# Second block: the norms of queries and keys and the decay's scalars between the projection's products

## What is computed

```python
def hybrid_layer(x, ln1_g, w_in, q_norm_g, k_norm_g, rpb, ...):
    h = rms_norm_2(x, ln1_g)
    proj = h @ w_in                                # 3*512 attention, 4*512 delta rule, 16 scalars
    aq, ak, av, dqkv, dz, dab = jnp.split(proj, ...)
    aq = rms_norm_2(hs(aq), q_norm_g)              # per head of 64
    ak = rms_norm_2(hs(ak), k_norm_g)
    attn = rms_norm_2(neighbourhood_attention(aq, ak, hs(av), rpb), attn_out_g)
    dn = bidirectional_gated_deltanet(dqkv, dz, dab[:, :, 0], dab[:, :, 1], conv_w, ...)
    x = x + jnp.concatenate([attn, dn], axis=-1) @ w_out
    return x + hierarchical_moe(rms_norm_2(x, ln2_g), ...)

# inside the delta rule's mixer
    qkv = silu(conv(qkv_raw, width 5, per channel))
    q = l2_norm(q) * 128 ** -0.5; k = l2_norm(k)   # per head of 128
    g = -exp(a_log) * softplus(a + dt_bias); beta = sigmoid(b)
    o = rms_norm_2(gated_delta_rule(both directions), out_norm_g) * silu(z)
```

## Time and profile before

| | us |
|---|---|
| median of 3 runs | 2851.36 |
| lowest, highest | 2849.64, 2853.24 |
| the profiled execution | 2852.15 |
| span in its profile | 2850.4 |
| mean granted clock over the span | 0.858 |
| PE busy | 2314.1 (81%) |
| DVE busy | 1195.0 (42%) |
| ACT busy | 855.3 (30%) |
| POOL busy | 190.0 (7%) |

### The profile page before, as it was taken

One profiled execution on the slowest core, in us unless ns is written; L12 is line 12 of the kernel. 1 busy time (PEld: TensorE's weight loads), 2 busy tenths in 40 slices (PEclk: granted clock), 3 DMA queues, 4 the chain that ended last, 5 costly groups with the idle time before them and its releaser, 6 DMA issues. The chain is left out here.

```text
span 2850.4 us, 32608 instructions
## 1 busy us (share of the span) xinstructions
PE 2314.1 (81%) x13804; PEld 1694.5 (59%) x13804; DVE 1195.0 (42%) x1868; ACT 855.3 (30%) x1270; POOL 190.0 (7%) x190
## 2 busy tenths in 40 slices
PE   7889999958964667679999979867688588888884
PEld 5768888837822667458888858646676533333331
DVE  3346664374158444546664344434524411111112
ACT  4324443264242222334443243464103210101000
POOL 0000000000004111000000000000220011111100
PEclk9889999979986666789999989965757699999997
DMA  4112232222200110122222223210104199999996
GB/s 182 60 59 89 89 104 82 95 76 97 79 0 4 18 15 13 60 74 76 102 98 87 98 72 119 84 28 1 23 1 164 78 388 419 416 408 407 401 396 233
DMA packets 106597, 377.27 MB, mean 132 GB/s; under 512 B 54960, under 2 KB 55744, under 8 KB 67536
## 3 DMA queue, kind: packets, MB, share of 16 engines
q1 hardware_dynamic: 84848, 296.44, 28.1%
q10 hardware_dynamic: 9216, 67.11, 5.7%
q0 software_dynamic: 12384, 11.58, 1.4%
HBM read 375.31 MB, written 27.53 MB: 141 GB/s over the span
## 5 line engine op out<-in xcount | busy, mean ns | idle before, releaser
L579 PE MATMUL ps<-xh,wh 128*128 128x512 f32 x1384 | 552.8, 399 | 85.9 <-DVE wl L546 35.9
L580 PE MATMUL ps<-xl,wh 128*128 128x512 f32 x1384 | 548.1, 396 | 0.0
L581 PE MATMUL ps<-xh,wl 128*128 128x512 f32 x1384 | 547.4, 396 | 0.0
L546 DVE TENSOR_TENSOR wl<-raw,wh 128x2048 fp32r<-128x2048 f32 (+2 forms) x127 | 264.4, 2082 | 326.4 <-ACT wh L540 326.4
L579 PEld LDWEIGHTS ps<-xh,wh 128*128 128x128 f32 x1384 | 266.1, 192 | 159.7 <-issue 55.3
L2959 PE MATMUL ps<-egu,XT 128*64 128x512 f32 x1088 | 272.1, 657 | 84.5 <-DMA egu<-e_up 80.1
L581 PEld LDWEIGHTS ps<-xh,wl 128*128 128x128 f32 x1384 | 265.6, 192 | 56.4
L580 PEld LDWEIGHTS ps<-xl,wh 128*128 128x128 f32 x1384 | 266.4, 192 | 54.9
L540 ACT ACTIVATE wh<-raw 128x2048 fp32r<-128x2048 f32 (+2 forms) x127 | 220.3, 1735 | 82.7 <-PE ps L864 69.3
L2959 PEld LDWEIGHTS ps<-egu,XT 128*64 128x64 f32 x1088 | 94.8, 151 | 238.3 <-issue 222.3
L2977 DVE TENSOR_TENSOR HIDT<-ps,SIL 128x256 f32<-128x256 f32 x34 | 14.4, 424 | 350.1 <-ACT SIL L2969 350.1
(11 more groups left out here) (460 smaller groups left out, 3385.7 us busy)
## 6 DMA issues: line engine op xcount, KB each, us to landing
egu<-e_gate SPq DMA_DIRECT2D x68, 1024.0 KB, 14.5
egu<-e_up SPq DMA_DIRECT2D x68, 1024.0 KB, 25.5
ed<-e_down ACTq DMA_DIRECT2D x64, 1024.0 KB, 9.7
raw<-up SPq DMA_DIRECT2D x44, 1024.0 KB, 4.8
raw<-down SPq DMA_DIRECT2D x32, 704.0 KB, 4.0
raw<-rwkv_rkv SPq DMA_DIRECT2D x12, 1024.0 KB, 4.8
raw<-in_dn SPq DMA_DIRECT2D x8, 1024.0 KB, 4.8
raw<-sgu_u SPq DMA_DIRECT2D x4, 1024.0 KB, 8.3
```

What stands on the lines that cost most here:

```text
L546: e.tensor_tensor(K.WL[s][:, 0:n], K.RAW[r][:, 0:n], K.WH[s][:, 0:n].bitcast(F32), SUB).then_inc(*K.w_low.mark(i))
L579: e.matmul(o, h[:, q, k], x_high[:, k], start=k == 0, stop=False)
L580: e.matmul(o, h[:, q, k], x_low[:, k], start=False, stop=False)
L581: last = e.matmul(o, l[:, q, k], x_high[:, k], start=False, stop=k == KT - 1)
```

## The change

- PE: the 8 norm products of queries and keys stand between the two value chunks; the 16 scalar columns come before the delta tiles; the transposes of the scalars after delta tiles 0 and 1; the 8 norm products of the delta rule's q and k after tile 11; the decay's products between tiles 13 and 14. Tiles 12 to 15 (the gate) come last.
- ACT: the square of a query or key tile follows its copy; the 8 logarithms stand between the two value chunks, the 8 exponentials after them; the square of a delta q or k tile follows its silu; sigmoid and two exponentials stand after tile 4; all other logarithms and exponentials between tile 11 and the gate.
- DVE: the norm of query or key tile m follows the convolution of tile m; the scalars' first steps follow tile 2, the rest stands before the norms of the delta rule's q and k.
- The squares have rooms of their own (`square_room`), in buffers that are filled later; the convolutions turn over 5 temporary tiles in place of 6.
- SP and POOL: bias tile 0 has another room and is loaded after the first query tile; bias tiles 1 to 3 and the second half of the values' tiles wait for delta tile 15, the last product.
- `gemm_pe` and `gemm_tok_pe` can make a part of a stage's tiles.

```diff
@@ weights, uses
         feed("in2_v", 2048)
+        feed("in2_ab", 1024)
         feed("in2_dn", 2048)
-        feed("in2_ab", 1024)
...
-                        ("n_fin", 1), ("n_ln1", 1), ("in2_qk", 8), ("in2_v", 8), ("in2_dn", 16), ("in2_ab", 2),
-                        ("sq_qk", 8), ("sq_kq", 8), ("dn_sc", 1)):
+                        ("n_fin", 1), ("n_ln1", 1), ("in2_qk", 8), ("in2_v0", 4), ("sq_qk", 8), ("in2_v1", 4), ("in2_ab", 1), ("in2_dn", 2),
+                        ("ab_turned", 1), ("in2_dn2", 10), ("sq_kq", 8), ("in2_dn12", 2), ("dn_sc", 1), ("in2_dn14", 2)):
@@ layer2_sp, layer2_pool
+    e.wait_ge(*K.gemm_sum("in2_qk", 0))
+    load_bias(K, e, 0)
     load_weights(K, e, K.first["in2_dn"], K.first["out2"])
-    e.wait_ge(*K.gemm_sum("in2_ab", 0))
-    for b in range(4):
+    e.wait_ge(*K.gemm_sum("in2_dn", 15))
+    for b in range(1, 4):
+        load_bias(K, e, b)
...
         if b == 2:
-            e.wait_ge(*K.gemm_sum("in2_ab", 0))
+            e.wait_ge(*K.gemm_sum("in2_dn", 15))
@@ layer2_pe
     gemm_pe(K, e, "in2_qk", "in2_qk", 8, K.XH, K.XL)
-    gemm_tok_pe(K, e, "in2_v", "in2_v", 2, 256, "in2_qk")
-    gemm_pe(K, e, "in2_dn", "in2_dn", 16, K.XH, K.XL, ready="in2_qk")
+    gemm_tok_pe(K, e, "in2_v", "in2_v", range(1), 256, "in2_qk")
+    squares_pe(K, e, "sq_qk", "blk")
+    gemm_tok_pe(K, e, "in2_v", "in2_v", range(1, 2), 256, "in2_qk")
     gemm_pe(K, e, "in2_ab", "in2_ab", 1, K.XH, K.XL, mt=1, ready="in2_qk")
+    gemm_pe(K, e, "in2_dn", "in2_dn", 2, K.XH, K.XL, ready="in2_qk")
...
+    gemm_pe(K, e, "in2_dn", "in2_dn", 10, K.XH, K.XL, ready="in2_qk", begin=2)
+    squares_pe(K, e, "sq_kq", "ones")
+    gemm_pe(K, e, "in2_dn", "in2_dn", 2, K.XH, K.XL, ready="in2_qk", begin=12)
...
+    gemm_pe(K, e, "in2_dn", "in2_dn", 2, K.XH, K.XL, ready="in2_qk", begin=14)
@@ layer2_act
+        e.wait_ge(*K.act_out("in2_qk", m))
+        e.activation(square_room(K, "sq_qk", m), K.QK[:, m], ACT.Square).then_inc(*K.square.mark("sq_qk", m))
...
+    values(0)
+    factors_ln_act(K, e, "sq_qk")
+    values(1)
+    factors_exp_act(K, e, "sq_qk")
+    next_high(K, e, K.first["in2_ab"])
...
         e.activation(dst, z, ACT.Silu).then_inc(*K.act_out.mark("in2_dn", m))
+        if m < 8:
+            e.wait_ge(*K.act_out("in2_dn", m))
+            e.activation(square_room(K, "sq_kq", m), of_kq(K, m), ACT.Square).then_inc(*K.square.mark("sq_kq", m))
+        if m == 4:
+            e.wait_ge(*K.dve_delta("abs"))
+            e.activation(K.sc["BE"][:, :, :, :], of_ab(K, 1), ACT.Sigmoid).then_inc(*K.act_delta.mark("beta"))
+            e.activation(flat(K, "SC2"), flat(K, "SC2"), ACT.Exp, scale=-1.0).then_inc(*K.act_delta.mark("exp"))
...
+    factors_ln_act(K, e, "sq_kq")
+    factors_exp_act(K, e, "sq_kq")
@@ layer2_dve
         K.board.empty(u, K.conv("in2_dn", m, 3))
+        if m < 8:
+            e.wait_ge(*K.rstd("sq_qk", m, "r"))
+            e.scalar_tensor_tensor(K.QK[:, m], K.QK[:, m], K.prm("qg" if m < 4 else "kg"), square_room(K, "sq_qk", m), MUL, MUL).then_inc(
+                *K.normed.mark("sq_qk", m))
```

More of the change, by code:

```diff
@@ L556, in next_low, with gemm_pe @@
         weight_low(K, e, i + 1)
-def gemm_pe(K, e, name, stage, nm, x_high, x_low, mt=2, at=0, ready=None):
-    for i in range(nm // mt):
+def gemm_pe(K, e, name, stage, nm, x_high, x_low, mt=2, at=0, ready=None, begin=0):
+    use = K.u[stage if begin == 0 else f"{stage}{begin}"] - begin
+    for i in range(begin // mt, (begin + nm) // mt):
         item = K.first[name] + at + i
@@ L573, in gemm_pe @@
             for q in range(mt):
-                u = K.u[stage] + mt * i + q
+                u = use + mt * i + q
                 o = K.ps[:, u % 8]
@@ L587, in gemm_tok_pe @@
 def gemm_tok_pe(K, e, name, stage, chunks, cols, ready):
-    for ch in range(chunks):
+    for ch in chunks:
         item = K.first[name] + ch
@@ L1837, in layer2_pool, with squares_pe @@
             e.dma_start(K.AVB[b][:, half], src).then_inc(*K.v_in[b].landing(b, half))
+def squares_pe(K, e, name, of):
+    for m in range(8):
+        u = K.u[name] + m
+        for t in K.board.emptied(u - 8):
+            e.wait_ge(*t)
+        e.wait_ge(*K.square(name, m))
+        e.matmul(K.ps[:, u % 8], K.cst(of, 128), square_room(K, name, m), start=True, stop=True).then_inc(*K.norm_sum.mark(name, m))
 def layer2_pe(K, e):
@@ L1871, in layer2_pe, with ab_room, square_room, dn_use @@
     e.matmul(K.ps[:, b, 96:128], K.cst("half", 128, 128), GG, start=True, stop=True).then_inc(*K.delta_sum.mark("decay"))
+    gemm_pe(K, e, "in2_dn", "in2_dn", 2, K.XH, K.XL, ready="in2_qk", begin=14)
 def of_kq(K, m):
     return K.KQ[:, 1 - m // 4, m % 4]
+def ab_room(K):
+    return K.GT[0:16, 0].rearrange("p a b -> p (a b)")
+def square_room(K, name, m):
+    if name == "sq_qk":
+        return K.DV[:, m] if m < 4 else K.ZG[:, m - 4]
+    if m < 4:
+        return K.AT[:, m]
+    if m < 6:
+        return K.GT[:, m - 4].rearrange("p a b -> p (a b)")
+    return K.EX[:, :] if m == 6 else K.T[5]
+def dn_use(K, m):
+    at = 0 if m < 2 else 2 if m < 12 else 12 if m < 14 else 14
+    return K.u[f"in2_dn{at}" if at else "in2_dn"] + m - at
+def factors_ln_act(K, e, name):
+    for m in range(8):
+        u = K.u[name] + m
+        e.wait_ge(*K.norm_sum(name, m))
+        e.activation(square_room(K, name, m), K.ps[:, u % 8], ACT.Ln, bias=K.prm("eps"), scale=1.0 / 64 if name == "sq_qk" else 1.0).then_inc(
+            *K.rstd.mark(name, m, "ln"))
+        K.board.empty(u, K.rstd(name, m, "ln"))
+def factors_exp_act(K, e, name):
+    for m in range(8):
+        x = square_room(K, name, m)
+        e.wait_ge(*K.rstd(name, m, "ln"))
+        e.activation(x, x, ACT.Exp, scale=-0.5).then_inc(*K.rstd.mark(name, m, "r"))
 def layer2_act(K, e):
@@ L1947, in layer2_act @@
     e.activation(K.EH[:, :, :].rearrange("p a b -> p (a b)"), K.ps[:, b, 64:128], ACT.Exp).then_inc(*K.act_delta.mark("eh"))
+    K.board.empty(K.u["dn_sc"], K.act_delta("eh"))
     e.activation(flat(K, "EG"), flat(K, "GC"), ACT.Exp).then_inc(*K.act_delta.mark("eg"))
     e.activation(flat(K, "ED"), flat(K, "GL"), ACT.Exp).then_inc(*K.act_delta.mark("ed"))
+    for m in range(12, 16):
+        u = dn_use(K, m)
+        e.wait_ge(*K.gemm_sum("in2_dn", m))
+        e.wait_ge(*K.normed("sq_qk", m - 8))
+        e.activation(K.ZG[:, m - 12], K.ps[:, u % 8], ACT.Silu).then_inc(*K.act_out.mark("in2_dn", m))
+        K.board.empty(u, K.act_out("in2_dn", m))
     K.board.point("ACT", "attn")
@@ L1977, in layer2_dve @@
         next_low(K, e, K.first["in2_v"] + i)
-    for m in range(16):
+    next_low(K, e, K.first["in2_ab"])
+    u = K.u["in2_ab"]
+    e.wait_ge(*K.gemm_sum("in2_ab", 0))
+    e.tensor_copy(ab_room(K), K.ps[0:16, u % 8]).then_inc(*K.dve_out.mark("in2_ab"))
+    K.board.empty(u, K.dve_out("in2_ab"))
+    full = {k: K.sc[k][:, :, :, :] for k in K.sc}
+    for m in range(12):
         if m % 2 == 0:
             next_low(K, e, K.first["in2_dn"] + m // 2)
-        if m >= 12:
-            continue
-        u = K.u["in2_dn"] + m
-        z, o = K.T[m % 6], K.ps[:, u % 8]
+        u = dn_use(K, m)
+        z, o = K.T[m % 5], K.ps[:, u % 8]
         e.wait_ge(*K.act_out("in2_dn", m, "tap"))
@@ L2019, in layer2_dve @@
+    next_low(K, e, K.first["in2_dn"] + 6)
     e.wait_ge(*K.act_delta("ln"))
```

124 lines of the change are left out of this document (43 added, 81 removed).

## The result

The changed kernel takes **2826.37 us** (median of 4 executions, 2809.28 to 2829.09); the kernel before takes 2851.23 on the same chip. The ratio is 0.990, 95% interval 0.986 to 0.994. The profiled execution took 2829.09 us (span 2827.3), so it is 2.7 above the median.

What follows compares the result with a forecast made beforehand. It took a serial norms stretch before attention, and ACT and DVE pacing the projection, as the bounds. -58.5 + 16.8 PE work + 28.1 waits + 4.6 clock - 2 attention = -11.0, so 2840.5 us; range 2832.5 to 2848.

Steps and rivals of the forecast that it cites:

- the last term: Attention's start: PE arrives at full clock, so the first 4 us of its work run faster; -2 us, bounds 0 and 4.
- Rival B: Attention stays at full clock: -21 us in place of -2, 2822 us in all; chance 0.07.
- The serial stretch taken away: Norms and decay between projection and attention, 50.6 us, go, with 7.9 us of old projection waits; together -58.5 us.
- Ring of 13.5 per pair: Projection of the delta rule's features: squares lengthen the ACT and DVE cycle per tile pair by 1.34, to 13.5 us.
- Rival A: In the projection, the squares don't lengthen the ACT and DVE cycle: -17.9 us, 2833 us in all; chance 0.06.
- The pair with three loads: Behind tile 4, sigmoid, two exponentials and three table loads add 4.5 us, making that pair 18.0 us, PE wait 7.2.
- Ring waits, 15.1: Projection: PE's waits at tile pairs lengthened by squares, small activations and table loads; together 15.1 us.
- Clock, +4.6 for three falls: Projection: PE's clock falls to 0.50 at three long waits, 1.5 us each; +4.6 us.
- Norm products, 13.9: 16 norm products return to PE between the projection's products at 0.87 us each; 13.9 us.
- Decay 2.3: The decay's small products return to PE between the projection's products; 2.3 us.
- C: Rival: the pauses of each pair lose PE's clock in the projection; +38 us, 2879 in all; chance 0.05.
- D: Rival: no change to speak of; the projection's cycle grows 1.3 us more per pair; -2.6 us, 2848.5 in all; chance 0.10.

Runs made afterwards that it cites:

- after_kept_warm: Changed kernel with 8 extra PE products without use in the pause ahead of each of attention's first three blocks' row transposes; 2807.89 us.
- after_cold: Changed kernel with 12 more silus of the last gate tile on ACT, 8 us in which PE idles ahead of attention; 2844.40 us.
- after_decay_last: Changed kernel with the decay's products and the three following exps put back behind the gate's last tiles; 2832.49 us.
- before_warm: Kernel before with 20 PE products without use between the last norm product and the wait for the decay's rates; 2845.77 us.
- before_carried: Kernel before with 22 PE products without use ahead of the decay's products and 4 between these and attention; 2843.96 us.
- after_ring_short: Changed kernel with ACT's sigmoid and two exps moved from behind tile 4 to behind the casting of tile 12's weights; 2827.24 us.
- after_norms_twice: Changed kernel with each of the 16 norm products issued twice; 2833.35 us.
- after_again: The changed kernel run once more without an edit, for its spread; 2828.04 us, one execution of six at 2805.65.
- after_filled_waits: Changed kernel with PE products without use in the projection's waits ahead of several delta tiles and the keys' last norm product; 2829.39 us.

## Why the prediction was wrong

**The step that failed** is the last term, "I take 2; bounds 0 and 4" for attention's start. It measured 10.75 us. The value was taken from the earlier trace rows, where a stretch of small products lost the clock near 979 us with PE busy 2.09 of 3.40 us. Attention after the change is busy 15.07 of 23.50, about the same share, and kept it. The row was read as a property of sparse products in general; it was one place, with other shapes (64x64 and 128x64). And the bounds weren't bounds: "the first 4 us of its work" had no row behind it. From the rows that were shown, the block of 34.27 us up to the pause of 3.93 and PE's busy share of 82% gave a price for the whole block at full clock: half of 0.82 x 34.3 = 28 us of PE work at most, 14, and that was the upper bound to put in.

**Rival B** named the mechanism with 0.07: full clock up to the first long pause. Its sign came true: attention's clock is 0.61 over the 105 us from 1879. I had held the fall near 979 against it. The Trainium skill ("TensorE: Matmul & The Clock Gate", section "Why this matters for your kernels") says that PE-idle gaps over some 3 us bring the clock down. Here the trace agrees at the first pause (4.36 us: clock lost; filled: clock kept, after_kept_warm), and in after_cold (8.24). It isn't the whole: the clock was also lost in or right behind waits of 1.62, 1.70 and 2.17 us in after_decay_last, before_warm and before_carried, so the absence of a long gap is no promise. My doubt had that much ground; the value and the bounds that I drew from it had none. B's own price, 21 us more, was too large, as it took all of attention; only the first block stays warm, 10.75.

**The forecast sum without that term** was -9.0 at attention's start; measured -13.0 there, -13.7 from the stage's start, and -13.2 from there with attention entered at full clock in both. Its steps:

- *The serial stretch taken away, -58.5*: held. Nothing of it is left in the stage rows.
- *Ring of 13.5 per pair*: 13.52 and 13.51. Right, and after_ring_short shows the ring by moving what is in it. Rival A is out. *The pair with three loads, 18.0*: 16.70; the third load (1806.52) lies under a convolution of DVE.
- *Wait before the first delta tiles, 4.8*: 4.72. *Keys' last product, 2.8*: 2.48. *Tile 12, 4.5*: 3.63. *End, 0.9*: 0.69. Right within a microsecond each.
- *Ring waits, 15.1*: 8.5 (2.28 + 0.73 + 5.52). With them the waits are 20.1, not 28.1. *Clock, +4.6 for three falls*: there were four stretches at 0.50, of 3.4, 3.4, 6.8 and 6.8 us. These two terms count one thing twice: where the ring paces, PE at 0.50 works into its own wait, so the waits are shorter and the falls nearly free. With most of the falls filled away (the clock at 0.99) the stage got 1.2 us shorter, and 1.6 came from the first fall alone, which stands outside the ring. There were more falls than I had, and so the double count and the miscount partly cancel.
- *Norm products, 13.9*: the queries' half is on the path (after_norms_twice: 6.8 us for eight more, 0.85 each). The keys' half has 6.1 us of waits right behind it, which it could have been set against. *Decay 2.3*: 1.0 (1866.13 to 1867.16), since it now runs at full clock.
- The 4.7 us by which the stage came out better are then 1.3 (the third load), 1.3 (decay) and 1.5 (the four small waits), and 0.6 in what doesn't cancel above. This split is an estimate; only the loads, the norm products and the clock falls were moved by a run of their own.
- *Bias and value tiles cost nothing*: right. DMA share is 0.70 in the first 23.5 us of attention, and no wait of PE names them. PE is idle 0.69 us between the stages, as forecast under 2.
- *C, slower by a lost clock in the projection*: the clock does fall there, 4 times. The first fall costs 1.6 us, near the 1.5 of the forecast, and the one behind tile 4 nothing, for the reason above; what the last two cost no run shows one by one. *D* is out by the 13.5.
- Small slips that change nothing: 2851.36 - 11.0 is 2840.4, not 2840.5, and the sum without falls, -17.6, is 2833.8, while the range starts at 2832.5.

So with the fills in both kernels the change is worth 9.7 us. That this is near the 11 forecast is luck: 2 of the 11 were the clock, the stage was some 4 too dear, and 3.5 of what the stage gave is lost elsewhere. What was missed is a state that one stage hands to the next: the change took away 50 us in which PE was busy 24 and waited up to 9.81 us at a time, and the stage behind it inherited the clock. That two executions (2809.28 here, 2805.65 in after_again) were some 20 us shorter still is another matter. Neither was profiled. The recurrence's clock is the likely cause, as in the one profile that shows it; attention keeping the clock in those executions would give about as much and isn't excluded for these two. Why the clock rises in some executions stays open.

## What to carry to other kernels

When a change takes away a stretch in which PE waits, price the stage behind it at full clock up to its first long pause, from its own rows, and write that down as a bound, however small the chance. Don't add the price of a clock fall to a wait that another engine sets. And look for the longest PE wait ahead of each stage that runs at 0.50: 18 products without use there gave more (29 us) than the whole rearrangement.

## What the hardware showed that I had not expected

- PE busy 20.00 of 20 us with the recurrence's small products (64 to 128 columns) stayed at 0.50 in the kernel before; entered at full clock, the same products held 1.00 for 46.8 us with PE busy 39.6. In 13 of the 14 profiles the level went with the wait ahead of them: 0.50 throughout with the 9.55 us open, 1.00 throughout with 8.04 us of products in it. In before_warm the wait was open and the clock rose in the fourth chunk all the same.
- The same wait of 2.17 us in attention left the clock at 1.00 in the changed kernel (1892.70), cost 3.4 us of it in after_kept_warm (near 1911) and lost it in before_carried (near 1905). Of the profiles that came to it at full clock in the new order without a fill there, after_filled_waits and after_norms_twice lost it too (1891.1 for 3.4 us, 1897.1 for the rest of the block). The wait's length alone doesn't tell.
- Eight extra products of 128x512 behind the keys' norms made the stage 1.8 us shorter.
